# Two transformer blocks in two-part fp32: low weight parts stored in the raw weights' buffer

## What is computed

```python
# first block
h = rmsnorm(x, g_attn);  proj = h @ w_in             # 2048 x 6144 (+ 8 columns)
mixed = attentions(proj)
x = x + mixed @ w_out                                # 2048 x 2048
u = relu(rmsnorm(x, g_mlp) @ w_up)                   # 2048 x 8192
x = rmsnorm(x + (u * u) @ w_down, g_final)           # 8192 x 2048
# second block
proj = rmsnorm(x, g) @ w_in_2                        # 2048 x 7168 (+ 16 columns)
h = x + recurrences(proj) @ w_out_2                  # 2048 x 2048
hn = rmsnorm(h, g2);  qry = hn @ w_query             # 2048 x 2048
# per head: top 16 of 128 keys in each half, top 16 of their 256 sums, softmax -> gate
hid = gelu(hn . u_tab[e]);  h = h + sum_e gate_e * hid_e * v_tab[e]
out = rmsnorm(h, g_final2)
```

## Time and profile before

| what | value |
|---|---|
| median of three runs | 3610.48 us (3607.24 to 3612.63) |
| the profiled execution's own time | 3605.09 us |
| its span in the profile | 3603.3 us |
| TensorE busy, matmuls | 3412.4 us, 95% of the span |
| VectorE busy | 1926.7 us, 53% |
| ScalarE busy | 1450.4 us, 40% |
| GpSimd busy | 406.9 us, 11% |
| loads of raw weights | 536 of 1 MB; 604.21 MB read from HBM in all, 178 GB/s moved |
| mean granted clock of TensorE | 0.965 of full |

### The profile page before, as it was taken

One profiled execution on the slowest core, in us unless ns is written; L12 is line 12 of the kernel. 1 busy time (PEld: TensorE's weight loads), 2 busy tenths in 40 slices (PEclk: granted clock), 3 DMA queues, 4 the chain that ended last, 5 costly groups with the idle time before them and its releaser, 6 DMA issues.

```text
span 3603.3 us, 49923 instructions
## 1 busy us (share of the span) xinstructions
PE 3412.4 (95%) x20466; PEld 3008.1 (83%) x20466; DVE 1926.7 (53%) x1885; ACT 1450.4 (40%) x1241; POOL 406.9 (11%) x420
## 2 busy tenths in 40 slices
PE   7998799999999999976589999999999999999998
PEld 5887689999999878864478999999999988888886
DVE  3443555555555654445555688655554555555554
ACT  4334544333333443332323444444444433333333
POOL 0000100000000000012440000366662000000000
PEclk9997899999999999977689999999999999999999
DMA  6552155555555555510005555565666665666663
GB/s 241 188 189 83 49 187 187 187 186 186 186 188 187 185 191 189 190 49 1 1 1 191 174 202 211 193 234 203 213 210 223 257 238 233 233 233 233 233 238 123
DMA packets 129578, 641.93 MB, mean 178 GB/s; under 512 B 12576, under 2 KB 45728, under 8 KB 60192
## 3 DMA queue, kind: packets, MB, share of 16 engines
q1 hardware_dynamic: 96400, 622.07, 48.5%
q10 hardware_dynamic: 33040, 17.83, 1.8%
HBM read 604.21 MB, written 35.65 MB: 178 GB/s over the span
## 4 chain that ended last, share of the span: by engine, by line
PE 48%; DVE 1%; ACT 1%; issue 1%; DVEq 0%; POOL 0%; ACTq 0%; POOLq 0%
PE pj L258 7%; PE pj L259 7%; PE pj L260 7%; PE pj L246 4%; PE pj L244 4%; PE pj L245 4%; PE pt L245 2%; PE pt L246 2%; PE pm L245 2%; PE pm L246 2%; PE pm L244 2%; PE pt L244 2%; PE pm L1640 1%; PE pj L1241 1%; ACT hi L229 1%
## 5 line engine op out<-in xcount | busy, mean ns | idle before, releaser
L233 DVE TENSOR_TENSOR lo<-raw,hi 128x2048 fp32r<-128x2048 f32 x536 | 1228.6, 2293 | 1272.6 <-ACT hi L229 1271.0
L229 ACT ACTIVATE hi<-raw 128x2048 fp32r<-128x2048 f32 x536 | 1026.9, 1917 | 1686.3 <-PE pj L246 748.6
L258 PE MATMUL pj<-xh,hi 128*128 128x256 f32 x3328 | 937.6, 282 | 8.3 <-DVE lo L233 8.3
L259 PE MATMUL pj<-xl,hi 128*128 128x256 f32 x3328 | 931.1, 280 | 0.0
L260 PE MATMUL pj<-xh,lo 128*128 128x256 f32 x3328 | 930.6, 280 | 0.0
L258 PEld LDWEIGHTS pj<-xh,hi 128*128 128x128 f32 x3328 | 627.9, 189 | 9.3 <-DVE lo L233 8.6
L259 PEld LDWEIGHTS pj<-xl,hi 128*128 128x128 f32 x3328 | 627.7, 189 | 0.7
L260 PEld LDWEIGHTS pj<-xh,lo 128*128 128x128 f32 x3328 | 627.6, 189 | 0.0
L244 PE MATMUL pj<-hi,xh 128*128 128x512 f32 x1088 | 434.2, 399 | 20.7 <-DVE lo L233 20.7
L245 PE MATMUL pj<-lo,xh 128*128 128x512 f32 x1088 | 432.5, 398 | 0.0
L246 PE MATMUL pj<-hi,xl 128*128 128x512 f32 x1088 | 432.4, 397 | 0.0
(11 more groups left out here) (375 smaller groups left out, 3713.5 us busy)
## 6 DMA issues: line engine op xcount, KB each, us to landing
raw<-w_peer SPq DMA_DIRECT2D x256, 1024.0 KB, 6.0
raw<-w_mlp SPq DMA_DIRECT2D x128, 1024.0 KB, 4.8
raw<-w_in SPq DMA_DIRECT2D x104, 1024.0 KB, 4.9
raw<-w_out SPq DMA_DIRECT2D x32, 1024.0 KB, 4.8
raw<-w_q SPq DMA_DIRECT2D x16, 1024.0 KB, 4.8
act_scratch<-hidU SPq DMA_DIRECT2D x32, 512.0 KB, 2.9
gates_scratch<-stage ACTq DMA_DIRECT2D x8, 2048.0 KB, 17.1
hidV<-act_scratch SPq DMA_DIRECT2D x32, 512.0 KB, 3.7
```

The lines of the kernel that those rows point to most:

```text
L229: nc.scalar.activation(hi[:, j, :], raw[:, j, :], ACT.Copy).then_inc(hi_ready, 1)
L233: nc.vector.tensor_tensor(lo[:, j, :], raw[:, j, :], hi[:, j, :].bitcast(F32), ALU.subtract).then_inc(lo_ready, 1)
L258: nc.tensor.matmul(o, hi[:, j, cols], xh[:, k0 + k, :], start=clears, stop=False, skip_group_check=True)
L259: nc.tensor.matmul(o, hi[:, j, cols], xl[:, k0 + k, :], start=False, stop=False, skip_group_check=True)
```

## The change

`lo` is placed at the address of `raw` (same size, same slots), so `make_lo` writes its result over the raw weights it reads. A raw slot may then be loaded again only when TensorE has read `lo`, so that the load of chunk c waits for `pe_used >= c - 3` (TensorE has ended chunk c - 4) where it waited for `lo_ready >= c - 3`. This holds for all loads from chunk 4 on. No instruction is added, removed or moved on any engine; one semaphore in SP's waits is another. All tensors behind `raw` and `hi` lie 32 KB per partition lower.

```diff
+        at_raw = cursor[0]
         raw = sb("raw", [P, SLOTS, CH])
+        lo = sb("lo", [P, SLOTS, CH], F32R, at=at_raw)
         hi = sb("hi", [P, SLOTS, CH], F32R)
-        lo = sb("lo", [P, SLOTS, CH], F32R)
...
                         if not (isinstance(i, int) and q0 + i == 0):
-                            sp.wait_ge(lo_ready, (i + q0) * SLOTS + j - 3)
+                            sp.wait_ge(pe_used, (i + q0) * SLOTS + j - 3)
                         sp.dma_start(raw[:, j, :], src).then_inc(raw_ready[j], 16)
...
             def peer_chunk(q, s, j):
-                sp.wait_ge(lo_ready, q * SLOTS + j - 3)
+                sp.wait_ge(pe_used, q * SLOTS + j - 3)
```

## The result

The changed kernel takes 3850.61 us (median of four runs, 3847.02 to 3852.76) beside 3608.86 us for the kernel before. The ratio is 1.0671 with a 95% interval of 1.0658 to 1.0685: 242 us slower. The forecast was 3840, with a range of 3770 to 3905. The ratios of the experiments are against repeats of the kernel before from their own session (near 3605 us), without one of them that took 4104 us at a low granted clock.

What follows compares the result with a forecast made beforehand. TensorE, busy for 95% of the span, was taken to bound the kernel. Terms of 146 + 28 + 49 + 8 + 6 - 6 = 231 us on the time before gave 3840 us, with a range of 3770 to 3905.

Steps and rivals of the forecast that it cites:

- term 2: Turns with gates: loads beside the eight 2 MB gate writes land later, +28 us (bounds 10 and 43).
- Term 1: Turns with gates: `hotA` queued behind the later `lo` stalls TensorE, +146 us; E(c) is chunk c's end on TensorE.
- Term 3: Turns with gates: the clock drops behind three in four of 32 stalls, +49 us (bounds 0 and 80).
- Term 4: MLP, third down turn: the add, behind `lo` and `coefficients_lo`, comes 0.5 us too late; 15 groups, +8 us.
- Term 5: Ends of input projections, +6 us; two long idle times at loop ends partly overlap with new stalls, -6 us.
- the cover of 16.8 us for the weights: `lo` of chunk c+3 is due 16.8 us after TensorE ends chunk c-1 but comes at 9.2; most stages cost nothing.
- Rival (c): Whole kernel: cover holds everywhere, not slower, 3605 to 3612 us; chance 0.05.
- (a): Turns with gates: stalls spread over the turns at 2 us each, the clock holds, about 3790 us; chance 0.27.
- (b): MLP and gates: a load alone takes 5.6 us rather than 4.9, all four adds late, about 3893 us; chance 0.15.

Runs made afterwards that it cites:

- e9: The changed kernel with `scale_up` behind `hotA` and the 0.5 MB activation write issued behind a block's third load instead of its fourth: 3833.22 us, ratio 1.0622.
- e3: The changed kernel with `scale_up` behind `hotA` instead of ahead of it in the first turn of blocks with gates: 3840.24 us, ratio 1.0634.
- e6: The changed kernel with 16 added matmuls ahead of TensorE's wait for `hotA` in each of the 64 turns with gates: 3811.04 us, ratio 1.0573.
- e5: The changed kernel with `coefficients_lo` behind the add in the third down turn of the MLP: 3837.06 us, ratio 1.0644.
- e2: The changed kernel with `hot_group` (the one-hot tiles) ahead of `make_lo` in VectorE's turns with gates: 3627.04 us, ratio 1.0060.

## Why the prediction was right

The sign, the place and the mechanism were right, and the time was within 11 us. That it came so near is in part luck: term 2 was some 24 us too high, and terms 1, 3, 4 and 5 together more than that too low. The terms fared as follows.

- **What bounds the kernel, and the cover of 16.8 us for the weights:** right. PEER down is the same to 0.1 us, and its loads land in 4.8 us where they had 7.5; 5 to 6 was forecast. Rival (c), no loss, is out: no load is near 0.8 us.
- **Term 1, +146:** right in its chain, slightly short. E(c+1) = E(c-1) + 17.0 has a stall of 4.0 in it, and 3.8 to 4.5 is what stands there. With `scale_up` I had 5.1 and the change mostly shows 5.9 to 6.5: the missing 1.1 us is the activation write, which slows the load ahead of it from 4.8 to 6.0 us and which the prediction left out. e9 removed just that much. Measured, the stalls sum to 160, the first one ahead of the stretch included.
- **Term 2, +28 for loads beside gate writes:** far too high. It priced the writes by the earlier trace rows, where loads came one after the other at all times. With the new pattern there are gaps, and up to 2820 a write of 9 to 12 us falls into one, and no stall is longer for it. Behind 2820 the mechanism of the term is there: loads of 10.4 and 8.7 us come before stalls of 5.1 and 7.1 where 3.9 was usual, so some 4 us in all. (Its 8.3 us for a load has no row; the rows have 8.6 and 10.2.) The activation write, 1.1 us in each of the 13 blocks up to 2820 or some 14 us, took its place and hid a part of the error.
- **Term 3, +49 for the clock:** right in kind, short in size: 69. I had put it at three drops in four; every one of the 32 stalls of 3.8 us or more had slow matmuls behind it, and a turn behind a stall lost 2.2 us, near the 2.05 read from the earlier trace rows. The full count of 66 was the better estimate. The stalls alternate, but not for the reason given, so that part was luck: e3 and e9 equalised the two chains and they alternated on. A likelier reason is that a slow chunk lies in the chain that stalled, and keeps it the slower one; e6, where the clock mostly holds, has fewer long stalls, which agrees but doesn't prove it. Another, that two equal chains simply keep whatever lag they start with, wasn't tested either.
- **Term 4, +8 in the MLP:** right in place and mechanism, measured 13.7. The stall before the first up chunk was 0.41 to 0.92, where I had 0.5. The idle times sum to 8.6 us; the other 5, about 0.3 us a group, are not explained, though e5 takes most of the 13.7 away.
- **Term 5:** a net 0 was forecast, and no other stage was to grow by over 3 us; the stages outside the MLP and gates lost 17 us, and two of them 7.2 and 6.0. 4.6 of it are one place that I had read as covered, the second input projection, where TensorE's one wait for `lo` grew from 2.16 to 6.78 us; 5.9 are the wait for the first `hotA`, which the 160 of term 1 hold as well. Nothing was run on these. The -6 for the two long idle times of the earlier trace rows was too little: they are gone with 8.3 us of idle time and 4 to 5 of slow work, against 3.6 of new idle time at loop ends.
- **Rivals (a) and (b):** the clock did not hold, and MLP loads land in 4.9 us as before. The upper end of the range, 3905, doesn't follow from its working: 3840 + 15 + 31 is 3886, and (b) is 3893.

## What to carry to other kernels

A buffer freed later is not priced by how long the data itself can wait, but by what stands behind its next use on an engine that works in order: here weights had 7.6 us to spare, and small tiles queued behind them had none. Look for the operation in the same turn that is due first, and put it ahead of the one that is due three chunks later; that took 220 us off the changed kernel and even 8 off the one before. And price the clock too: here each stall of TensorE of 4 us or more cost 2 us more in slow matmuls behind it.

## What the runs showed of the hardware

- **A short idle time costs more than itself.** Stalls of 3.8 to 7.1 us were each followed by gate matmuls of 1.8 to 2.1 us instead of 1.05. The granted clock of the stretch fell to 0.84, and matmuls nobody needs made the program 35 us faster. The Trainium skill (TensorE: Matmul & The Clock Gate, Part 1: The HAM clock gate) says that idling throttles the clock and activity releases it; e6 agrees, with 0.96.
- **A transfer issued behind another can slow it.** A 1 MB load, followed after 0.5 to 0.6 us by a 0.5 MB write from the same queue, took some 6 us to land (6.1 for the one at 2613.36) instead of 4.8 to 4.9, about once a block. In e9 the write was moved behind another load, and the slow landing moved with it.
- **GpSimd's `hotB` took different times in different kernels.** The same 256 operations took 1083 ns each in the kernel before, 912 in e2, 774 in the change and 672 in e6. The busy share of VectorE alone doesn't order them: in the turns with gates it is 54% both in the kernel before and in e2. The cause wasn't looked for. The group of the changed kernel, from its page:

```profile
L1823 POOL TENSOR_SCALAR hotB<-cst,slot_c 128x128 f32<-128x128 f32 x256 | 193.9, 774 | 443.9 <-PE pm L1641 443.7
```
